# Low weight parts of two subtiles in one VectorE instruction, at the odd subtile's place in VectorE's order

## The reference, cut to what matters

```python
mod = (c_act @ w_ada[i] + b_ada[i])[:, None, :]
sh_a, sc_a, g_a, sh_m, sc_m, g_m = jnp.split(mod, N_MOD, axis=-1)
h = x * (1.0 + sc_a) + sh_a
y = diff_attention(h, ...)               # layer 0; layer 1: sliding_window_attention(h, ...)
x = layer_norm(ALPHA * x + (1.0 + g_a) * y, ln_mix_g[i], ln_mix_b[i])
h = x * (1.0 + sc_m) + sh_m
y = jnp.square(jax.nn.relu(h @ w_up[i])) @ w_down[i]
x = layer_norm(ALPHA * x + (1.0 + g_m) * y, ln_mlp_g[i], ln_mlp_b[i])
```

## Time and profile before

| | |
|---|---|
| median of 3 runs | 2262.32 us (2262.31 to 2262.47) |
| profiled execution, its own time | 2259.59 us |
| its span, first to last instruction | 2257.8 us |
| TensorE busy | 2186.4 us |
| VectorE busy | 1645.7 us, of it 851.6 us in 712 low parts |
| ScalarE busy | 988.2 us |
| mean granted TensorE clock | 0.994 |

### The profile page before, as it was taken

How to read it: one execution, slowest core, us unless ns; L and a number is a source line. 1 busy time by engine, 2 the same in 40 slices (tenths; PEclk the granted TensorE clock), 3 DMA queues, 4 the chain that set the end, 5 groups by cost and what they waited for, 6 DMA issues and landing times.

```text
span 2257.8 us, 25954 instructions
## 1 busy us (share of the span) xinstructions
PE 2186.4 (97%) x10076; PEld 1811.8 (80%) x10076; DVE 1645.7 (73%) x1742; ACT 988.2 (44%) x1334; POOL 34.0 (2%) x53
## 2 busy tenths in 40 slices
PE   6899999999999999999999899999999999999997
PEld 6777888887888888888887688877888888888885
DVE  5888888787887786787687888885664555464557
ACT  0134444446433443443444556536433544343442
POOL 0000000000000000000000000000000000000000
PEclk9999999999999999999999999999999999999999
DMA  9988888867998998899866755565666666666672
GB/s 375 385 302 323 314 312 302 303 236 268 335 333 299 331 332 314 291 353 327 321 236 215 242 205 191 196 218 184 229 226 214 212 228 203 214 219 227 220 228 102
DMA packets 253583, 596.41 MB, mean 264 GB/s; under 512 B 13378, under 2 KB 14740, under 8 KB 253204
## 3 DMA queue, kind: packets, MB, share of 16 engines
q1 hardware_dynamic: 244688, 578.86, 73.2%
q10 hardware_dynamic: 8772, 15.89, 2.2%
HBM read 592.60 MB, written 2.10 MB: 263 GB/s over the span
## 4 chain that ended last, share of the span: by engine, by line
PE 89%; DVE 6%; DMA 2%; issue 1%; ACT 1%; ACTq 0%; POOL 0%; DVEq 0%; POOLq 0%
PE pair L1594 24%; PE pair L1596 24%; PE pair L1595 24%; PE pair L1864 1%; DVE acc L859 1%; PE pair L1866 1%; PE pair L1865 1%; PE turn L1488 1%; DVE w_lo L837 1%; PE pair L1614 1%; PE turn L1938 1%; PE turn L1919 1%; PE pair L1616 1%; PE pair L1615 1%; PE pair L1724 1%
## 5 line engine op out<-in xcount | busy, mean ns | idle before, releaser
L837 DVE TENSOR_TENSOR w_lo<-raw,w_hi 128x1024 fp32r<-128x1024 f32 x712 | 851.6, 1219 | 255.8 <-ACT w_hi L470 249.1
L470 ACT ACTIVATE w_hi<-raw 128x1024 fp32r<-128x1024 f32 x712 | 729.2, 1059 | 595.2 <-PE pair L1596 409.0
L1594 PE MATMUL pair<-w_hi,h_hi 128*128 128x512 f32 x1456 | 581.1, 399 | 3.3 <-DVE w_lo L837 3.3
L1596 PE MATMUL pair<-w_hi,h_lo 128*128 128x512 f32 x1456 | 568.7, 391 | 0.0
L1595 PE MATMUL pair<-w_lo,h_hi 128*128 128x512 f32 x1456 | 567.5, 390 | 0.0
L1594 PE MATMUL pair<-w_hi,f_hi 128*128 128x512 f32 x1056 | 413.8, 392 | 0.0
L1596 PE MATMUL pair<-w_hi,f_lo 128*128 128x512 f32 x1056 | 411.1, 389 | 0.0
L1595 PE MATMUL pair<-w_lo,f_hi 128*128 128x512 f32 x1056 | 410.8, 389 | 0.0
L859 DVE SCALAR_TENSOR_TENSOR acc<-ada_w,cvec,acc 128x1024 f32<-128x1024 f32 x300 | 383.4, 1278 | 0.1
L1594 PEld LDWEIGHTS pair<-w_hi,h_hi 128*128 128x128 f32 x1456 | 273.9, 188 | 60.0 <-DVE w_lo L837 4.2
L1596 PEld LDWEIGHTS pair<-w_hi,h_lo 128*128 128x128 f32 x1456 | 273.5, 188 | 58.4
(11 more groups left out here) (188 smaller groups left out, 1641.3 us busy)
## 6 DMA issues: line engine op xcount, KB each, us to landing
ada_w<-in_w_ada_dram SPq DMA_DIRECT2D x320, 512.0 KB, 6.0
raw<-in_w_up_dram SPq DMA_DIRECT2D x128, 1024.0 KB, 5.5
raw<-in_w_down_dram SPq DMA_DIRECT2D x128, 1024.0 KB, 5.2
raw<-in_a_w_qkv_dram SPq DMA_DIRECT2D x48, 1024.0 KB, 7.4
ada_f<-in_w_ada_dram SPq DMA_DIRECT2D x44, 512.0 KB, 10.9
raw<-in_b_w_qkv_dram SPq DMA_DIRECT2D x20, 1024.0 KB, 5.3
raw<-in_a_w_o_dram SPq DMA_DIRECT2D x16, 1024.0 KB, 6.2
raw<-in_b_w_o_dram SPq DMA_DIRECT2D x16, 1024.0 KB, 5.1
```

What stands on the lines that cost most here:

```text
L470: act.activation(w_hi[:, (b.n * SUB + n) % SPLITS], raw[:, slot, k:k + 2], ACT.Copy).then_inc(hi_ready, 1)
L837: dve.tensor_tensor(w_lo[:, slot, k:k + 2], raw[:, slot, k:k + 2], w_hi[:, (b.n * SUB + n) % SPLITS].bitcast(F32), ALU.subtract).then_inc( ...
L1594: pe.matmul(o, hi[:, kt, at], w[:, k], start=kt == 0, stop=False)
L1596: mm = pe.matmul(o, lo[:, kt, at], w[:, k], start=False, stop=kt == KT - 1)
```

## The change

Where `block_` covers both subtiles of an even-odd pair, nothing is done at the even n, and at the odd n one instruction computes both: 2048 columns. It waits until `hi_ready` counts the odd subtile and raises `lo_ready` by 2. What else is due at the even n (`before`, `beside`, `later`, `ada_tile`, `hooks`) stays there. Single instructions are left where `block_` is called for one subtile of the pair alone (the first two blocks in part), in the norms for n = 0 to 5, and in blocks 13 and 54, whose quarters lie in another order. 335 pairs replace 670 of the 712 instructions; 42 stay single.

```diff
+            def split_lo_pair(n):
+
+                b = st.block
+                slot, k = raw_place(b.n, n)
+                first = (b.n * SUB + n) % SPLITS
+                dve.wait_ge(hi_ready, b.at(0, SUB) + n + 2)
+                dve.tensor_tensor(w_lo[:, slot], raw[:, slot],
+                                  w_hi[:, first:first + 2].rearrange("p a k n -> p (a k) n").bitcast(F32),
+                                  ALU.subtract).then_inc(lo_ready, 2)
+
...
                 for n in range(n0, n1):
-                    split_lo(n)
+                    if n - n % 2 < n0 or n - n % 2 + 1 >= n1 or st.block.n in PAIRED_SECOND:
+                        split_lo(n)
+                    elif n % 2 == 1:
+                        split_lo_pair(n - 1)
                     if before and n == at:
```

## The result

The changed kernel takes **2304.79 us** (median of 3 runs, 2302.47 to 2304.92) against 2262.32: a ratio of 1.0183, 95% interval 1.0168 to 1.0198. It is slower by 42.5 us. Forecast were 2298 us, between 2283 and 2310. The profiled execution took 2302.47 us with a span of 2300.7, so span grew by 42.9 us over that of the earlier trace rows.

A forecast was written before the change was run, and what follows sets the result against it. TensorE bounds the kernel (89% of the path); VectorE's saved time is idle, and late low parts cost. Nine terms sum to 35.6 us, taking the profiled 2259.6 to 2295.2; median forecast 2298 us, range 2283 to 2310.

The forecast's parts named there:

- Term 1: Seven blocks with a long `before` at n = 2: third subtile late, 2.30 us each, less shorter n = 6 waits; +15.4 us.
- Term 2: Tail block 15: pairs (2,3) and (4,5) late, pair (6,7) behind the modulation sum, 2.7 lost there; +4.4 us.
- Term 3: Up blocks: pair (4,5) ready after TensorE wants n = 4, 0.30 us in 28 of 32 blocks; +8.4 us, least certain.
- Terms 4, 6, 9: Norm blocks 16 and 57, +2.2 us; blocks 14 and 55 with hooks, +1.1; first low part at the start, +1.1.
- Term 7: Attention: VectorE's work at odd n behind a wait at even n moves 1.06 us later; +2.4 us.
- term 8: Up blocks 19 to 21 of layer 0, with affine steps and up to six tiles: n = 0 late; +1.8 us.
- term 5: Norm block 48 and after: lateness vanishes in the key's rope wait, query's rope comes 1.0 earlier; -1.2 us.
- the clock falls too: Rival, 13%: each 2.3 us wait of terms 1 and 2 drops TensorE to 1.2 GHz, 9 x 1.5 = 13 more, 2311 us.
- Only the long waits count: Rival, 15%: no restart for overlapped low parts and pairs ready before 2.28 us; terms 3, 8 go, 7 halves; 2286 us.
- VectorE's orders gain more: Rival, 3%: modulation tiles, ropes and sums come 1.1 us earlier at even n, gaining more than is lost; 2258 us.
- Margins cover all: Rival, 4%: TensorE in fact needs low parts later than its starts show; time stays 2262 us.
- a longer chain: Rival, 3%: a late block makes VectorE late for the next; 2320 us and above.

The follow-up runs named there:

- the ropes: Kernel before, low parts single, query rope's last steps ahead of n = 4's low part in blocks 50 to 53, one affine step behind key's rope: 2262.21 us.
- the kernel with seven pairs: Kernel before with pairs only for n = 2, 3 of blocks 45, 46, 47, 56, 86, 87, 88, at the odd place: 2278.59 us, ratio 1.0073.
- the kernel with the tiles and one rope: Kernel before, four modulation tiles moved out of blocks 48 and 49, affine step behind key's rope, query rope's steps ahead in block 50 only: 2257.49 us.
- all ropes: Kernel before, four modulation tiles moved out of blocks 48 and 49, affine step behind key's rope, query rope's steps ahead in blocks 50 to 53: 2258.26 us.

## Why the prediction was right, and where it was off

The sign, the mechanism and the sizes of nearly all terms hold; the time came out 6.8 us above the forecast and inside the range. Point by point:

- *Price of a pair.* 2.28 us forecast, 2.287 measured. The Trainium skill (VectorE: DVE Perf Modes, The TRN2 errata) gives 2291 ns for the addition of two 32-bit float tensors with 2048 columns. The trace agrees within 0.2%, on a subtraction. That page's advice to minimize the number of operations (Rules for kernel authors) shows in VectorE's busy time, 22 us less; by it alone the kernel would have gained, and it lost 42.5.
- *Ready less needed, plus 0.16.* The form held, and the restart was a little small. The third subtile starts 2.26 or 2.27 us later, fourteen times in two kernels, and the fourth another 0.13 to 0.18 where the clock stays: 2.40 to 2.44 us instead of 2.30. Rows 5 were read for one step; the matmuls behind it follow at 0.24 instead of 0.23 us for a while.
- *Term 1.* Seven blocks cost 16.6 without the clock, instead of 15.4. The small part was wrong: that each tail's wait for n = 6 falls by 0.25. It grew by 0.11 in block 47 and fell by 0.20 in 88, because the tail's own later pairs use up the reserve; in 56 it took up what the clock had lost. Undoing these pairs and block 15 gave 20.7 back.
- *Term 2.* 4.4 and, without the clock, 4.6. The step thought worst was worst: 2.72 us at n = 6.
- *Term 3.* 0.30 forecast, and 28 of 32 blocks hit, as said. The measured shift is 0.33 to 0.35 each, 9.5 in all instead of 8.4, again by the matmuls behind the restart.
- *Terms 4, 6, 9* within 0.2 us. *Term 7* 3.2 instead of 2.4, at the four places with little margin; *term 8* 2.4 instead of 1.8; *term 5* -2.1 instead of -1.2. In the kernel before the slow stretch stood in block 49; with the change it stands in block 48 instead, which the term left out.
- *The clock.* The step that failed is the choice between "the clock falls too" and "it does not" for all places at once; the sum had nothing for it. It fell behind five of nine waits for low parts of over 2 us. Three of these falls, in blocks 15, 46 and 87, cost 1.4, 1.6 and 1.6 us, 4.6 of the 8.3 us by which the shifts exceed the sum; the one in block 56 was made up at n = 6, and the one in block 48 had stood in 49 before. Most of the rest is term 1 without the clock (1.2), term 3 (1.1) and terms 7 and 8 (1.4), less 0.9 in term 5. That rival's price of 1.5 was right, its count was not: terms 1 and 2 name eight waits of this length and not nine, which makes 12 us and 2310, and three of the eight cost anything. The time came to lie between the sum and this rival, and inside the range.
- *The other rivals.* "Only the long waits count" falls with the singles in the up blocks (8.4 us). "VectorE's orders gain more" was real at two places but small: 2.6 us in the changed kernel's trace (blocks 49 and 50), and tried alone it gave nothing. "Margins cover all" and "a longer chain" found no row.

Of the signs that the prediction named, the 28 short waits stand in the weight loads' view and not in the matmuls', the wait at 1303 is gone altogether, and the one at 1281 is not: 1.1 us are left.

What stays open: what decides whether the clock falls behind a given wait of 2.1 us. The runs show only that it differs between kernels at the same block.

## What to carry to other kernels

Joining two instructions of a producer that is off the path saves time nobody waits for, and makes the first half late by the second half's duration, or by a whole wait if one stood between them: price it at the few consumers that wait for it, not by the producer's busy share. Seven of 335 joined instructions made over a third of the loss, and 216 at early places cost nothing. Before such a change ask for the smallest margin between ready and needed at each kind of place; and when a wait is taken away, look at which wait comes next, as the ropes showed.

## What was not expected of the hardware

- After one single wait of 2.10 to 2.56 us TensorE either kept its 2.4 GHz level (steps of 0.23 us) or ran seven steps of 0.43 us at 1.2 GHz, beginning 0.7 to 1.4 us behind the restart (499.59 to 500.26 in block 15, 1179.21 to 1180.58 in the kernel with seven pairs, where six steps followed). In the earlier trace rows a wait of 1.44 left it alone; one of 1.85 in block 50 of the kernel with the tiles and one rope was followed by five such steps, one of 1.88 at the same place with all ropes by none. The Trainium skill (TensorE: Matmul & The Clock Gate, Why this matters for your kernels) says that the rate falls back when TensorE idles between bursts of matmuls. That row is about longer gaps than most of these; here the rate fell behind five of the nine waits of 2.1 to 3.4 us.
- A producer that is 0.14 us late leaves no wait in the matmuls' list, only in that of the weight loads, and costs 0.31 us: 0.20 by the first step, 0.11 by the next.
